# Second routing product from rows ahead of the layer norm, and a new order of gelu pieces, turns and quarters around a gated linear unit

## The reference, cut to what matters

```python
    hid = jax.nn.gelu(y.astype(x.dtype), approximate=False)
    val, gate = jnp.split(hid @ w_glu, 2, axis=-1)
    return val * jax.nn.sigmoid(gate)
...
        x = layer_norm(ALPHA * x + h, ln_g[i, 0], ln_b[i, 0])
...
    logits = (xt @ w_router).astype(jnp.float32) + b_router.astype(jnp.float32)
    top_v, top_i = lax.top_k(logits, TOP_K)
```

## Time and profile before

| | us |
|---|---|
| median of 3 runs | 1252.93 (1251.98 to 1253.33) |
| the profiled execution | 1258.34 |
| its span in the profile | 1256.5 |
| TensorE matmul busy | 1224.8 (97%) |
| VectorE busy | 609.6 (49%) |
| ScalarE busy | 231.1 (18%) |
| mean granted TensorE clock | 0.986 of full |

### The profile page before, as it was taken

One profiled execution on the slowest core, in us unless ns is written; L12 is line 12 of the kernel. 1 busy time (PEld: TensorE's weight loads), 2 busy tenths in 40 slices (PEclk: granted clock), 3 DMA queues, 4 the chain that ended last, 5 costly groups with the idle time before them and its releaser, 6 DMA issues.

```text
span 1256.5 us, 25396 instructions
## 1 busy us (share of the span) xinstructions
PE 1224.8 (97%) x11085; PEld 826.5 (66%) x11085; DVE 609.6 (49%) x1135; ACT 231.1 (18%) x487; POOL 100.9 (8%) x102
## 2 busy tenths in 40 slices
PE   8999999999999999999999999999999989999997
PEld 7878867899954467456545554555447547998443
DVE  1658445466898857663110111011174257656545
ACT  3362331222211104320100101010010032111000
POOL 1040024100000000002100000000143110000000
PEclk9999899999999999998999999999999999999999
DMA  9970804756554855629999999999996340535520
GB/s 329 358 247 2 268 1 102 170 152 181 156 205 172 157 88 188 265 103 404 405 407 416 417 407 407 419 412 406 376 330 209 121 148 1 191 145 194 187 88 33
DMA packets 121803, 291.09 MB, mean 232 GB/s; under 512 B 6324, under 2 KB 69280, under 8 KB 109440
## 3 DMA queue, kind: packets, MB, share of 16 engines
q1 hardware_dynamic: 109536, 269.30, 59.7%
q0 software_dynamic: 4832, 14.67, 4.0%
q10 hardware_dynamic: 7360, 6.03, 1.6%
HBM read 273.21 MB, written 16.78 MB: 231 GB/s over the span
## 4 chain that ended last, share of the span: by engine, by line
PE 92%; DVE 3%; ACT 2%; DMA 1%; issue 1%; SPq 0%; DVEq 0%; ACTq 0%
PE bank L2860 18%; PE bank L2619 10%; PE bank L2269 9%; PE bank L2877 9%; PE bank L3064 8%; PE bank L3102 7%; PE bank L2626 6%; PE bank L2282 5%; PE bank L2799 3%; PE bank L2241 3%; PE bank L2702 2%; PE bank L2951 1%; PE bank L2725 1%; DMA arena<-ffn_w 1%; PE bank L2471 1%
## 5 line engine op out<-in xcount | busy, mean ns | idle before, releaser
L2860 PE MATMUL bank<-arena 128*32 128x352 f32 x3072 | 230.4, 462 | 0.7 <-DVE arena L1530 0.7
L2860 PEld LDWEIGHTS bank<-arena 128*32 128x32 f32 x3072 | 104.1, 110 | 124.2 <-issue 123.0
L2269 PE MATMUL bank<-xT,arena 128*128 128x256 f32 x576 | 130.3, 386 | 1.3 <-ACT arena L1913 1.3
L2269 PEld LDWEIGHTS bank<-xT,arena 128*128 128x128 f32 x576 | 110.9, 195 | 17.0 <-ACT arena L1913 1.8
L1575 DVE TENSOR_TENSOR arena<-arena,bank 128x352 f32<-128x352 f32 x24 | 19.2, 801 | 204.4 <-PE bank L2860 204.4
L2877 PE MATMUL bank<-arena 128*32 128x256 f32 x2112 | 115.5, 379 | 0.0
L2877 PEld LDWEIGHTS bank<-arena 128*32 128x32 f32 x2112 | 70.8, 110 | 44.1 <-issue 2.2
L3102 PE MATMUL bank<-arena 128*128 128x512 f32 x224 | 96.7, 592 | 0.7 <-DVE arena L1727 0.7
L2619 PE MATMUL bank<-xT,arena 128*128 128x128 f32 x704 | 83.2, 275 | 0.5 <-DVE arena L1274 0.5
L2619 PEld LDWEIGHTS bank<-xT,arena 128*128 128x128 f32 x704 | 80.8, 192 | 2.0 <-issue 1.3
L2626 PE MATMUL bank<-arena 128*128 128x512 f32 x176 | 78.0, 594 | 0.0
(11 more groups left out here) (493 smaller groups left out, 1470.1 us busy)
## 6 DMA issues: line engine op xcount, KB each, us to landing
arena<-moe_w SPq DMA_DIRECT2D x64, 1408.0 KB, 16.1
arena<-moe_w SPq DMA_DIRECT2D x24, 1536.0 KB, 18.6
arena<-ffn_w SPq DMA_DIRECT2D x44, 512.0 KB, 6.6
arena<-w_up SPq DMA_DIRECT2D x8, 2048.0 KB, 9.4
arena<-w_down SPq DMA_DIRECT2D x8, 2048.0 KB, 7.6
arena<-gdn_w_in SPq DMA_DIRECT2D x7, 2048.0 KB, 18.7
arena<-ffn_w SPq DMA_DIRECT2D x11, 1024.0 KB, 4.9
slot_rows<-arena SPq DMA_DIRECT2D x1, 9600.0 KB, 54.0
```

The costliest lines, as they stand in the source:

```text
L2269: last = mm(bank[:, at:at + SEQ], w[:, k, P * m:P * m + P], x[:, k, :], start=(k == 0), stop=(k == KT - 1))
L2860: last = mm(banks[i][32 * q:32 * q + 32, 0:EW1], xg[:, t, EK * s + kk], w[:, kk, EW1 * q:EW1 * q + EW1], start=(s == 0 and kk == 0), stop= ...
```

## The change

- **Gelu pieces.** The turns of piece j - 1 are issued in the middle of `y_piece(j)` (before its third quarter). VectorE takes the copy of the last y piece, between its first two weight sums of the GLU; ScalarE has no fourth copy, and goes from gelu 1 to gelu 2 and 3.
- **First GLU products.** Products 1 and 2 of h = 0 are interleaved: three matmuls of 1, the first of 2, the fourth of 1, the rest of 2.
- **Logits of the second 128 tokens.** logits = rstd * (x W' - mean * colsum(W')) + colsum(b W) + b_router with W' = g * W_router (g and b of the layer norm along the channels). VectorE builds W', the product b * W and their sums over the eight channel blocks (five small operations); a matmul with a matrix of ones adds them over the partitions (`banks[0][:, 8:24]`). The rows are turned before they are normalised, as far as each part of them is done (counter `raw_rows`), both halves are copied to `xT` by ScalarE, and eight matmuls with W' follow. VectorE finishes the logits with two operations of 8 columns.
- **Turn order.** Quarter "4a" is ahead of the first logits, which stand between the two quarters. The ranking of the first tile stands between the quarters' VectorE work. The first half of the norm of the second tile waits until its rows are turned. Both gathers of the first tile are behind the second logits. The five `keep_warm` matmuls are gone, the later single one stays. The maxima and differences for the gates are taken behind the count of passes.
- **Loads.** g and b of that layer norm are also loaded as rows of `vrows` (16 rows more, two loads on GpSimd's queue), and the turn of `vrows` waits for them (`vecs_loaded` 96).

The diff, cut to its core:

```diff
+        w_sums, route_c = route_w[:, 128:144], route_w[:, 144:160]
...
+            for i, name in enumerate(("ln_g", "ln_b")):
+                pool.dma_start(vrows[109 + 8 * i:117 + 8 * i], A[name][1, 0:1].rearrange("a (t p) -> (a t) p", p=P)).then_inc(vecs_loaded, 16)
...
+            def raw_step(ins):
+                raw[0] += 1
+                ins.then_inc(raw_rows, 1)
+                dve.wait_ge(raw_rows, raw[0])
...
             g_sum(1, 0)
+            dve.wait_ge(ys_done, NPIECE)
+            dve.wait_ge(yt_done, NPIECE - 2)
+            V_.tensor_copy(y_sb[:, 1].rearrange("p s (d c) -> p d s c", c=GC),
+                           banks[5][:, :].rearrange("p (d s c) -> p d s c", d=4, s=SUB)).then_inc(ys_read, 1)
             g_sum(2, 0)
...
+            dve.wait_ge(small_loaded, 64)
+            for w, at_ in ((wg_router, 109), (wb_router, 117)):
+                last = V_.tensor_tensor(w, w_router, vecT[:, at_:at_ + 8, None].broadcast_to((P, KT, 8)), ALU.mult)
+            link(last)
+            for i, w in enumerate((wg_router, wb_router)):
+                last = V_.tensor_reduce(w_sums[:, 8 * i:8 * i + 8], w.rearrange("p k e -> p e k"), AX, ALU.add)
+            link(last)
+            raw_step(V_.tensor_scalar(w_sums[:, 0:8], w_sums[:, 0:8], -1.0, None, ALU.mult))
+
             def rank_experts(n):
 
                 dve.wait_ge(route_done, n + 1)
-                link(V_.tensor_tensor(logits[:, n], banks[2 * n][:, 0:8], router_b, ALU.add))
+                if n:
+                    link(V_.scalar_tensor_tensor(logits[:, n], route_c[:, 0:8], mv[:, n, 0:1], banks[5][:, 0:8], ALU.mult, ALU.add))
+                    link(V_.scalar_tensor_tensor(logits[:, n], logits[:, n], rstd[:, n:n + 1], route_c[:, 8:16], ALU.mult, ALU.add))
+                else:
+                    V_.tensor_copy(route_c[:, 0:8], banks[0][:, 8:16])
+                    V_.tensor_tensor(route_c[:, 8:16], banks[0][:, 16:24], router_b, ALU.add)
+                    link(V_.tensor_tensor(logits[:, n], banks[0][:, 0:8], router_b, ALU.add))
...
-                rank_experts(0)
                 flat = stats[:].rearrange("p n a b -> p (n a b)")
...
+                    if i:
+                        rank_experts(0)
...
-                    link(V_.scalar_tensor_tensor(r, r, ALPHA, v, ALU.mult, ALU.add))
+                    raw_step(V_.scalar_tensor_tensor(r, r, ALPHA, v, ALU.mult, ALU.add))
...
             last_quarters()
-            affine(2, 1)
+            dve.wait_ge(normw_loaded, 96)
+            last_half = [xres[:, 1, 512 * hf:512 * hf + 512] for hf in range(2)]
+            for hf in range(2):
+                dve.wait_ge(xt_tr, 4 * seen_xt[0] + 3 + hf)
+                last = V_.scalar_tensor_tensor(last_half[hf], last_half[hf], mv[:, 1, 0:1], norm_w[:, 0, 512 * hf:512 * hf + 512], ALU.subtract, ALU.mult)
+            seen_xt[0] += 1
+            link(last)
             pick_tokens(0)
-            take_x(1, (banks[4], banks[5]))
+            scalar_step()
+            link(V_.reciprocal(rstd[:, 1:2], rstd[:, 1:2]))
+            rank_experts(1)
+            for hf in range(2):
+                V_.scalar_tensor_tensor(last_half[hf], last_half[hf], rstd[:, 1:2], norm_w[:, 1, 512 * hf:512 * hf + 512], ALU.mult, ALU.add).then_inc(norm_done, 1)
             dve.wait_ge(norm_done, 12)
-
-
-            rank_experts(1)
+            pick_tokens(1)
+
+            link(V_.tensor_reduce(passes_f, banks[3][:, 8:16], AX, ALU.max))
+            link(V_.tensor_scalar(scratch1, passes_f, 2.0 * SLOTS, 0.0, ALU.is_gt, ALU.add))
+            link(V_.tensor_scalar(passes_f, passes_f, float(SLOTS), scratch1, ALU.is_gt, ALU.add))
+            V_.tensor_copy(passes[:, :], passes_f).then_inc(passes_ready, 1)
+
             for n in range(NT):
...
+                if j < NPIECE - 1:
+                    take_y(j)
...
+            for j, bank, counter in ((0, banks[6], xt_v), (1, banks[2], xt_a)):
+                act.wait_ge(xt_tr, 4 * seen_xt[0] + 3 + j)
+                nc.scalar.copy(xT[:, 4 * j:4 * j + 4, P:2 * P], four(bank)).then_inc(counter, 1)
+            seen_xt[0] += 1
             layer_norm(1)
-            take_x(1, (banks[4], banks[5]))
...
-            pe.wait_ge(vecs_loaded, 64)
-            transpose(banks[3][:, 0:109], vrows).then_inc(vec_tr, 1)
+            pe.wait_ge(vecs_loaded, 96)
+            transpose(banks[3][:, 0:125], vrows).then_inc(vec_tr, 1)
...
+                    if d == 2 and j:
+                        y_transposes(j - 1)
...
+            glu_product(1, 0, ks=(0, 1, 2))
+            glu_product(2, 0, ks=(0,))
+            glu_product(1, 0, ks=(3,))
+            glu_product(2, 0, ks=(1, 2, 3))
             for h in range(2):
-                for i in (1, 2, 5, 6, 3):
+                for i in (1, 2, 5, 6, 3) if h else (5, 6, 3):
...
             glu_product(7, 1)
+            glu_product(4, 1, slice(0, 256), g_bank[1]["4a"])
             need_x()
             pe.wait_ge(small_loaded, 64)
+            pe.wait_ge(raw_rows, 1)
+            mm(banks[0][:, 8:24], mat(C_ONE), w_sums, start=True, stop=True)
             token_major(banks[0][:, 0:8], xT, w_router, 0).then_inc(route_done, 1)
-            glu_product(4, 1, slice(0, 256), g_bank[1]["4a"])
             glu_product(4, 1, slice(256, 512), g_bank[1]["4b"])
...
-            keep_warm(banks[0], 5)
-            turn_x(xres, 1, 4, (banks[4], banks[5]))
+            for c in range(KT):
+                if c in (0, 4, 6):
+                    pe.wait_ge(raw_rows, {0: 2, 4: 3, 6: 4}[c])
+                last = transpose(four(banks[2 if c // 4 else 6])[:, c % 4], xres[:, 1, P * c:P * c + P])
+                if c % 4 == 3:
+                    last.then_inc(xt_tr, 1)
+            turned[0] += 1
+            for k in range(KT):
+                if k == 0:
+                    pe.wait_ge(xt_v, turned[0])
+                if k == 4:
+                    pe.wait_ge(xt_a, turned[0])
+                last = mm(banks[5][:, 0:8], xT[:, k, P:2 * P], wg_router[:, k], start=(k == 0), stop=(k == KT - 1))
+            last.then_inc(route_done, 1)
             mm(banks[3][:, 0:16].rearrange("p (a b) -> p a b", a=2), mat(C_ONE), chosen[:, 0, None, :].broadcast_to((P, 2, 8)),
                start=True, stop=False, skip_group_check=True)
             gather(0, 0)
-            need_x()
-            token_major(banks[2][:, 0:8], xT, w_router, 1).then_inc(route_done, 1)
             gather(1, 0)
```

49 lines of the change are left out of this document (24 added, 25 removed).

## The result

The changed kernel took 1244.68 us, the median of five runs (1242.24 to 1245.87), beside 1253.33 (1251.98 to 1257.79) for the kernel before on the same chip: ratio 0.9922, 95% interval 0.9908 to 0.9936. It is 8.65 us faster in the medians; 1244.9 was predicted. A second comparison gave 1246.08 against 1252.87, ratio 0.9955 (0.9938 to 0.9971), 6.8 us. The ratios of this text are not quotients of the medians: by them the gain is 9.8 us (8.0 to 11.5) the first time and 5.6 (3.6 to 7.8) the second. The two intervals of the same code just miss each other, so an interval holds for its own comparison, and 0.3% between two comparisons proves nothing.

What follows compares the result with a forecast made beforehand. TensorE was taken to bound the kernel, holding 92% of the chain that ends last. Gains of 1.55, 1.45 and 5.85 less a loss of 0.8 made 8.05 us, from 1252.93 to 1244.9, range 1242.0 to 1249.0.

Steps and rivals of the forecast that it cites:

- The gelu end: Ahead of the first GLU product: the twelfth gelu ends earlier, so TensorE begins at 505.4 instead of 506.94; gain 1.55 us.
- Its sign: Between the y pieces and the first GLU product, the changed profile shows no wait over 1 us.
- The half clock in the GLU: First GLU products: the fall to 1.2 GHz goes once the 2.67 us idle is split; gain 1.45 us, between 0 and 1.6.
- The smaller rival: GLU clock falls all the same, and tail hand-overs cost 2 more or the start 1 more: about 1247.5 us; chance 0.22.
- The tail: From the end of product 7 to the first expert product: 576.15 against 582.01, gain 5.85 us.
- The late table load: ScalarE in the tail: 1.28 us load behind its copies, root ending at 565.05; the ranking behind has 2 us to spare.
- The start: Two more GpSimd loads ahead of the turn of the vectors, landing at 9.3 to 9.4: loss 0.8 us, between 0 and 1.9.
- What the earlier start meets: Expert stage: loads follow TensorE's progress, so 8 us earlier everything slides and 19 us stay free for expert 1's first slab.
- the sign that the prediction named for being wrong: A wait for a DMA appearing in the expert stage of the changed profile.
- The sum: Whole kernel: 1.55 + 1.45 + 5.85 - 0.8 = 8.05 us gained, from 1252.93 to 1244.9.

Runs made afterwards that it cites:

- gelu_only: Kernel before with the turns of piece j-1 inside y piece j and VectorE copying the last piece, products 1 and 2 in a row; 1251.92 us, ratio 0.9978.
- after_again: The changed kernel measured once more with no edit; 1246.08 us, ratio 0.9955 to the kernel before.
- start_only: Kernel before plus only the two further vector loads and the wait for them, loaded rows unused; 1254.09 us, ratio 0.9999.
- after_late: Changed kernel with the turn of the vectors behind the first in-projection product; 1245.76 us, ratio 0.9949 to the kernel before.
- gated_only: Kernel before with quarter a ahead of the first logits and the first ranking between the quarters on VectorE; 1251.48 us, ratio 0.9976.
- tail_only: Changed kernel with its gelu part undone, keeping the new tail and start; 1248.43 us, ratio 0.9951 to the kernel before.
- before_glufill: Kernel before with three unread 512-column matmuls in TensorE's 2.67 us wait ahead of the first GLU product; 1251.48 us, ratio 0.9993.

## Why the prediction was right

**The gelu end**, 1.55 predicted, 1.40 measured, in both profiles of the change and in `gelu_only`. The steps are where they were put: VectorE's copy takes 0.70, no gelu waits for turns. Its sign, no wait over 1 us ahead of the first GLU product, was set too tight: `after_again` has one of 1.14 there, and the stretch is as long (20.06).

**The half clock in the GLU**, 1.45. The number came out (36.28 to 34.59), but the reason given for it, that an idle of 2.67 made the fall and its going ends it, is the step that doesn't hold as put. `gelu_only` falls without the wait, `start_only` doesn't with it. One sample of the clock was read as a property of the code. The smaller rival priced it at zero. By the counts above its mean lies between the two, (3/4 - 2/9) x 1.7 = 0.9, and fourteen profiles are few for that.

**The tail**, 5.85 predicted from the end of product 7, 5.8 measured (27.2 to 21.4); from the turns on, 6.0. Over all profiles the old tail scatters by 1.2 us (above), so the first decimal is partly luck. Laid on the times of before (8.2 later) the steps agree to 0.3: logits end at 558.5 (predicted 558.8), quarter b at 560.3 (560.5), ranking at 561.0 (561.0), ScalarE's second copy at 563.4 (563.4), its root at 565.0 (565.05), second logits at 564.6 (564.75), the first gather starts at 565.0 (565.2), the filler ends at 571.75 (571.75), the first expert product is at 576.2 (576.15). The filler ran at half clock, as taken. The late table load lay under VectorE's work, with nothing to spare: the root ended at 556.77, VectorE's place work at 556.74.

**The start**, 0.8 predicted. TensorE reached the in-projection 0.70 later behind its first matmul, `start_only` 0.75. The next 0.49 of the table is not the wait's: `after_late`, which has no such wait, has 106.88 there too, and `start_only` 106.31. The turn waited for `ln_b` until 9.18 (9.3 to 9.4 predicted). `after_late` gets the 0.8 back, which shows that the place of the turn costs it and not the loads. That none of it is given back later was assumed there and isn't shown: the times can't tell it. By the 2.0 us plus bytes that the Trainium skill, "DMA: Bandwidth & Descriptors", section "Anatomy of one DMA — SWDGE (gpsimd) path", gives for such a load there would have been no wait. The trace has one again, 5.2 us after the issue of `ln_b` at 3.97.

**What the earlier start meets.** Only the weights' slack was looked at there, and it held. The scatter was not looked at. The first silu of expert 0 in ScalarE's timeline, before and after:

```profile
606.46 0.55 ACT L2138 ACTIVATE arena<-bank,small 128x352 f32<-128x352 f32 x1 [7.46 <-PE bank L2860]
```

```profile
593.65 0.55 ACT L2182 ACTIVATE arena<-bank,small 128x352 f32<-128x352 f32 x1 [1.56 <-PE bank L2923]
```

Behind the landing ScalarE still waited 7.46 us for TensorE before, and 1.56 after. That is the spare time which the change used up; in `after_again` it was overdrawn, and TensorE waited 0.95 and then 0.56. That is the sign that the prediction named for being wrong, a wait in the expert stage that goes back to a DMA. This step was incomplete, and it sets a bound on any further gain in the tail.

**The longer half clock at the experts' start**, not predicted, cost 1.2 in this profile. Other profiles have 29.9 to 31.4 for this stretch with either tail (`gated_only` 31.28, `tail_only` 30.06), so it isn't put down to the change either. `before_glufill`, with the old tail and all its fillers, has one low stretch of the same length, 564.4 to 581.5.

**The sum.** 1.40 + 6.01 - 0.70 = 6.7 is what the order of the code accounts for in this pair of profiles. The rest of the profiled 12.8 is +1.87 in the GLU (1.69 of it in the 80 records, by the clock), -1.21 at the experts, +4.66 in the delta rule, and 0.26 - 0.49 + 1.01 - 0.01 = 0.8 in stretches that the change doesn't touch. The two comparisons of times, 8.65 and 6.8, stand on either side of the predicted 8.05. With the mean 0.9 for the clock the parts come to 7.6; that the first gain came within 0.6 of the forecast, with 1.45 of it resting on a reason that doesn't hold, is in part luck.

## What to carry to other kernels

Sum up the steps of the chain that ends last row by row; that predicted a 21 us tail to 0.1. A fall of the clock seen in one profile is a sample: put a price on it both ways, and take it out of a comparison of two profiles by comparing stages. And when a stage is made to start earlier, look at every transfer that it starts, not at the largest alone: here a 2 MB scatter moved into the stream of weights, took two to four times as long to land, and in four of seven profiles made TensorE wait 0.5 to 3.1 us.
